# PEER value rows: gathered as 32 picks of 4 tokens and summed by TensorE alone, in place of 8 picks of 128 tokens summed by TensorE and VectorE

## The chip, the cores and the metric

One core of a Trainium2 chip runs the whole program, a two-block network over 512 tokens, in one launch. The time is that of the device, in microseconds. Three runs of the kernel before gave 4364.2 us in the median (4360.43 to 4366.75). PE is TensorE, DVE is VectorE, ACT is ScalarE, POOL is GpSimd, SP is SyncE.

## The reference, cut to what matters

Everything that changes lies in the last stage, the PEER feed-forward of the second block. Per token it takes 16 experts in each of 8 heads, 128 picks, out of 16384, and needs one row of 1024 floats from each of two tables in HBM per pick:

```python
def peer_ffn(h, w_q, keys1, keys2, u, v):          # tokens in chunks of 128
    q = (hc @ w_q).reshape(-1, 8, 128)
    s1, s2 = q[..., :64] @ k1.T, q[..., 64:] @ k2.T           # 128 keys each
    v1, i1 = lax.top_k(s1, 16); v2, i2 = lax.top_k(s2, 16)
    cand_s = v1[..., :, None] + v2[..., None, :]              # 256 per head
    cand_i = i1[..., :, None] * 128 + i2[..., None, :]
    best_s, best_pos = lax.top_k(cand_s, 16)
    expert = take_along_axis(cand_i, best_pos)
    g = softmax(best_s)
    act = gelu(einsum('cd,chkd->chk', hc, u[expert]))         # first table
    return einsum('chk,chkd->cd', g * act, v[expert])         # second table
# after it: x + gate2 * peer, and the final rms norm
```

## The kernel before, in words

Up to about 2975 us the program runs the first block and the attention of the second. Then `peer_stage` runs until the end. It holds 512 tokens as 4 tiles (`TT`) of 128 tokens. A tile has 128 picks per token, in 16 groups (`NG`) of `B` = 8 picks. One indirect DMA, which GpSimd issues, brings one pick of 128 tokens: 128 rows of 4 KB, token p's row in partition p. Both tables need 512 of them, 1024 in all.

The rows land in `peer_ring`, which has 16 slots, used as 4 places of 4 picks. Half a group (q = 0 or 1, 4 picks) is the unit of the list `order`, which fixes the order of all gathers. Entry i of it uses place i mod 4, and `free(i)` lets GpSimd refill a place only when the readers of entry i - 4 are done.

- A "first" entry (table `peer_u`) is read by VectorE: `dot_rows` multiplies each row by the token's input and sums it into `acts` (L3412), one instruction for each pick.
- A "value" entry (table `peer_v`) is read by two engines. TensorE (`add_rows`, L3213) takes 3 of 4 picks: the stationary operand is a 128x128 diagonal matrix with the weights of that pick, which ScalarE makes (`make_diags`, L3314), and the two 512-wide halves of the row stream past it into two PSUM banks. VectorE (`sum_rows`, L3443) takes the fourth with a multiply-add into two other banks. In the last 3 groups VectorE takes two of four.

Both engines are in the path of `free` for value entries. Group n of the values follows group n + 6 of the first rows (`LEAD`), less where a step carries two value groups (`EXTRA`), so 3 value groups are left when the first rows are over. The weight of a pick is gate times gelu(dot), made by VectorE a group at a time (`weigh`, L3424).

Beside that run, in each engine's written order: at the start, the last projections and norms of tiles 1 to 3 and the first choice; the query products of tiles 1 to 3 (`later_query` 0 to 7, L3173), 0 to 3 ahead of the first value rows and 4 to 7 between them; the key scores of the next tile (`scores`, on TensorE, copied out by ScalarE in `take_scores`); and the choice of the next tile's experts on VectorE (`choose`, in pieces, `choose_on`). At a tile's end `finish` adds the two partial sums, multiplies by the gate, adds to h and normalises.

Of the kernel before, what the change touches and what calls it, by code (L numbers as in the profile page):

```python
# [14 lines left out]
F32 = mybir.dt.float32  # L15
# [30 lines left out]
N_PEER = 16384  # L46
PICKS = PEER_HEADS * PEER_K
# [78 lines left out]
class Signal:  # L126
# [29 lines left out]
    i_weighed i_picked x_cum_stored x_cum_loaded x_logits x_masked x_exps x_turned x_taken y_added0 y_added1 y_added3  # L156
    y_weighed0 y_weighed1 stored x_copied_dve x_copied_act x_summed x_set x_inverse
# [2274 lines left out]
class ExpertKeys:  # L2432


    def __init__(self, S, st):
        H, NK = PEER_HEADS, PEER_K
        self.S, self.G = S, Routing()
        self.G.expert = S.sb("peer_expert", [P, TT, PICKS], I32, st)
        self.G.gate = S.sb("peer_gate", [P, TT, PICKS], F32, st)
# [18 lines left out]
    def choose(self, t, h0, h1):  # L2458
# [54 lines left out]
        for side in range(2):  # L2513
# [12 lines left out]
        nc.vector.scalar_tensor_tensor(key[:, 0, hs, :], key[:, 0, hs, :], float(P), key[:, 1, hs, :], ALU.mult,  # L2526
                                       ALU.add).then_inc(own.sem, o.up())
        self.dve.wait_ge(own.sem, o.value())
        nc.vector.tensor_copy(self.G.expert[:, t, :].rearrange("p (h k) -> p h k", h=H)[:, hs, :], key[:, 0, hs, :]).then_inc(self.chosen.sem, 1)
# [430 lines left out]
def peer_stage(S, K, qT, h2, M, mix, w_out, out_gain, out):  # L2960
# [6 lines left out]
    N, LEAD, EXTRA = TT * NG, 6, (20, 24, 28)  # L2967
    LAG, SCORED = LEAD - len(EXTRA), LEAD + 3
    queries_at = {LEAD + 1: (4, 5), LEAD + 2: (6, 7)}
    queries_out_at = {LEAD - 2: (0, 1), LEAD - 1: (2, 3), LEAD + 1: (4, 5), LEAD + 2: (6, 7)}  # L2970
    exps = S.sig("u_exps")
    acted, diags, w_staged, fin, cleared = (S.sig("y_" + x) for x in ("acted", "diags", "w_staged", "fin", "cleared"))
    arrived = [S.sig(f"y_arrived{q}", pool_dma=True) for q in range(4)]
    dotted = [S.sig(f"y_dotted{q}") for q in (0, 1)]
    added = [S.sig(f"y_added{q}") for q in (0, 1)]
    weighed = [S.sig(f"y_weighed{q}") for q in (0, 1)]
# [22 lines left out]
    def dve_rows(n):  # L2999
        return (0, 4) if n < N - LAG else (0, 2, 4, 6)  # L3000

    def pe_rows(n):
        return [b for b in range(B) if b not in dve_rows(n)]

    def pe_rows_to(n):
        return sum(len(pe_rows(x)) for x in range(n))

    def dve_rows_to(n, q):
        return sum(b // Q == q for x in range(n) for b in dve_rows(x))

    steps = [([m], []) for m in range(LEAD)]
    n_value = 0
    for m in range(LEAD, N):
        more = 2 if m in EXTRA else 1
        steps.append(([m], list(range(n_value, n_value + more))))
        n_value += more
# [7 lines left out]
    def slot_of(kind, n, b):  # L3024
        return Q * (place[kind, n, b // Q] % 4) + b % Q
# [753 lines left out]
```

## Time and profile before

| | |
|---|---|
| median of 3 runs | 4364.2 us (4360.43 to 4366.75) |
| the profiled execution: span from first to last instruction | 4359.8 us |
| mean granted TensorE clock in it | 0.927 |
| PE busy | 3776.8 us (87%) |
| DVE busy | 1707.1 us (39%) |
| ACT busy | 628.1 us (14%) |
| POOL busy | 1097.7 us (25%) |
| bytes moved | 1092.57 MB, mean 251 GB/s |

The profile gives no time of its own for the profiled execution beside the span. The span lies 4.4 us below the median of the runs and 0.6 us below the fastest. The busy shares are means over stages with different limits; the stage that changes is the last third, in which GpSimd issues the gathers. A matmul of float32 operands shows as two records of MATMUL and two of LDWEIGHTS, called passes below.

### The profile page before, as it was taken

How to read it: one execution, taken by the hardware profiler on the slowest of the kernel's cores; microseconds unless marked ns; L12 is line 12 of the kernel's file. 1: busy time of each engine (PE TensorE's matmuls, PEld its weight loads, DVE VectorE, ACT ScalarE, POOL GpSimd, SP SyncE). 2: the span in 40 equal slices, each digit the busy share in tenths (PEclk: the TensorE clock that was granted, in tenths of full speed). 3: DMA queues.
4: the chain of work that ended last, by engine and by line, in shares of the span. 5: the costliest groups of instructions: out<-in, count | busy, mean ns of one | idle time of the engine just before them, and what ended most of it. 6: DMA issues, size and time to landing. Idle time of an engine off the chain costs nothing. (4 is left out here: it accounts for less than half of the span.)

```text
span 4359.8 us, 45503 instructions
## 1 busy us (share of the span) xinstructions
PE 3776.8 (87%) x17106; PEld 2506.1 (57%) x17106; DVE 1707.1 (39%) x3683; ACT 628.1 (14%) x1566; POOL 1097.7 (25%) x1162
## 2 busy tenths in 40 slices
PE   7989999998989999999999997998766767766676
PEld 3455777744747888888999993475322223222222
DVE  2052231013730000000000004748778776877655
ACT  1121000013520000000000003143211111111011
POOL 0010000001400000000000000004567777777775
PEclk9989999999989999999999998988888888888888
DMA  3143675230019888898777754026899999999998
GB/s 113 48 153 123 237 251 191 98 135 0 20 63 277 307 295 304 306 312 294 259 254 256 246 203 138 30 97 243 339 353 388 418 416 420 415 418 418 412 420 355
DMA packets 546999, 1092.57 MB, mean 251 GB/s; under 512 B 37497, under 2 KB 333830, under 8 KB 546742
## 3 DMA queue, kind: packets, MB, share of 16 engines
q1 hardware_dynamic: 393674, 539.66, 36.5%
q0 software_dynamic: 150768, 546.25, 31.2%
q10 hardware_dynamic: 2428, 5.03, 0.3%
q8 instruction: 69, 1.13, 0.1%
q14 instruction: 60, 0.49, 0.0%
HBM read 1069.55 MB, written 21.30 MB: 250 GB/s over the span
## 5 line engine op out<-in xcount | busy, mean ns | idle before, releaser
L3213 PE MATMUL banks<-peer_ring,consts 128*128 128x512 f32 x1512 | 843.7, 719 | 375.3 <-DMA peer_ring<-in_peer_v_dram,peer_expert 375.3
L3213 PEld LDWEIGHTS banks<-peer_ring,consts 128*128 128x128 f32 x1512 | 337.8, 231 | 876.2 <-DMA peer_ring<-in_peer_v_dram,peer_expert 468.0
L3412 DVE SCALAR_TENSOR_TENSOR peer_ring<-peer_ring,banks 128x1024 f32<-128x1024 f32 x512 | 594.1, 1218 | 254.0 <-DMA peer_ring<-in_peer_u_dram,peer_expert 253.0
L3117 POOL DMA_INDIRECT peer_ring<-in_peer_u_dram,peer_expert x512 | 484.9, 947 | 552.2 <-POOLq L2744 346.9
L3117 POOL DMA_INDIRECT peer_ring<-in_peer_v_dram,peer_expert x512 | 488.7, 955 | 182.7 <-issue 139.8
L2013 DVE TENSOR_TENSOR experts_hid<-experts_gs,banks 128x128 f32<-128x128 f32 (+1 forms) x224 | 66.7, 298 | 1175.9 <-ACT experts_gs L1983 1175.9
L1890 PEld LDWEIGHTS banks<-rows_xt,experts_wg 128*128 128x128 f32 x3584 | 446.9, 192 | 45.6 <-issue 45.4
L1890 PE MATMUL banks<-rows_xt,experts_wg 128*128 128x128 f32 (+1 forms) x3584 | 462.3, 282 | 11.8 <-DMA experts_wu<-in_moe_w_up_dram 9.7
L1890 PE MATMUL banks<-rows_xt,experts_wu 128*128 128x128 f32 (+1 forms) x3584 | 460.9, 282 | 0.0
L1890 PEld LDWEIGHTS banks<-rows_xt,experts_wu 128*128 128x128 f32 x3584 | 440.7, 192 | 0.0
L405 PE MATMUL banks<-xT,proj_w 128*128 128x512 f32 (+1 forms) x720 | 319.9, 602 | 8.1 <-PEq L3563 4.6
L1799 POOL DMA_DIRECT2D rows_index<-token_of_row x13 | 7.5, 577 | 1060.3 <-PE banks L1815 1042.6
L1907 PE MATMUL banks<-experts_wd,experts_hid 128*128 128x512 f32 x560 | 251.9, 592 | 0.0
L405 PEld LDWEIGHTS banks<-xT,proj_w 128*128 128x128 f32 (+1 forms) x720 | 135.6, 190 | 185.2 <-issue 183.8
L1023 POOL TENSOR_TENSOR hgrn_both<-k,hgrn_diff 128x256 f32<-128x256 f32 x56 | 44.4, 814 | 776.0 <-ACT hgrn_diff L934 761.5
L1983 ACT ACTIVATE experts_gs<-banks 128x128 f32<-128x128 f32 (+1 forms) x224 | 64.0, 286 | 1182.8 <-PE banks L1890 1182.8
L3443 DVE SCALAR_TENSOR_TENSOR banks<-peer_ring,peer_wgt,banks 128x1024 f32<-128x1024 f32 x130 | 167.4, 1288 | 89.2 <-DMA peer_ring<-in_peer_v_dram,peer_expert 88.6
L1920 PE MATMUL banks<-experts_hid,experts_wd 128*128 128x152 f32 x1344 | 180.5, 293 | 0.0
L1920 PEld LDWEIGHTS banks<-experts_hid,experts_wd 128*128 128x128 f32 x1344 | 176.3, 190 | 0.4
L408 PE MATMUL banks<-proj_w,xT 128*128 128x512 f32 (+1 forms) x448 | 174.1, 548 | 0.0
L1357 PE MATMUL banks<-xT,ffn_wg 128*128 128x256 f32 x704 | 161.2, 382 | 1.2 <-ACT ada_c L1395 1.2
L1431 DVE TENSOR_TENSOR ffn_hid<-ffn_gs,banks 128x256 f32<-128x256 f32 x44 | 18.5, 422 | 360.8 <-ACT ffn_gs L1401 360.8
(502 smaller groups left out, 3766.7 us busy)
## 6 DMA issues: line engine op xcount, KB each, us to landing
experts_wg<-in_moe_w_gate_dram SPq DMA_DIRECT2D x112, 1024.0 KB, 5.1
experts_wu<-in_moe_w_up_dram SPq DMA_DIRECT2D x112, 1024.0 KB, 7.6
experts_wd<-in_moe_w_down_dram SPq DMA_DIRECT2D x112, 1024.0 KB, 8.0
ada_w<-in_w_ada_dram SPq DMA_DIRECT2D x12, 2048.0 KB, 8.0
ffn_wg<-in_ffn_w_gate_dram SPq DMA_DIRECT2D x22, 1024.0 KB, 7.8
ffn_wu<-in_ffn_w_up_dram SPq DMA_DIRECT2D x22, 1024.0 KB, 10.4
ffn_wd<-in_ffn_w_down_dram SPq DMA_DIRECT2D x22, 1024.0 KB, 11.8
y_rows<-blank SPq DMA_DIRECT2D x1, 12288.0 KB, 42.6
```

The costliest lines, as they stand in the source:

```text
L405: last = nc.tensor.matmul(out_of(g), wk[:, m * P:m * P + width], xT[:, k, :], start=(k == 0), stop=(k == KD - 1))
L408: last = nc.tensor.matmul(out_of(g), xT[:, k, m * P:(m + 1) * P], wk[:, 0:n], start=(k == 0), stop=(k == KD - 1))
L1357: last = nc.tensor.matmul(ps[bank][:, 0:ROWS], w[:, b, k, j * P:(j + 1) * P], xT[:, k, u * ROWS:(u + 1) * ROWS], start=(k == 0), stop=(k = ...
L1890: ins = nc.tensor.matmul(ps[bank][:, 0:E.rows], w[:, b, k, j * P:(j + 1) * P], E.xu[:, k, :], start=(k == 0), stop=(k == KD - 1))
L1907: ins = nc.tensor.matmul(ps[hf][:, :], hid[:, j, 0:P], wd[:, b, j, hf * 512:(hf + 1) * 512], start=(first and j == 0), stop=(final and j = ...
L1920: ins = nc.tensor.matmul(ps[d // 2][:, at:at + B.rows], wd[:, b, j, d * P:(d + 1) * P], hid[:, j, :], start=False, stop=False, skip_group_ ...
L1983: nc.scalar.activation(gs[:, j, 0:E.rows], ps[4 + j][:, 0:E.rows], ACT.Silu).then_inc(E.gated[j].sem, 1)
L2013: nc.vector.tensor_tensor(hid[:, j, 0:E.rows], gs[:, j, 0:E.rows], ps[6 + j][:, 0:E.rows], ALU.mult).then_inc(E.hidden[j].sem, 1)
L3117: pool.indirect_dma_start(out=ring[:, slot_of(kind, n, b), :], out_offset=None, in_=tables[kind == "value"], in_offset=bass.IndirectOffset ...
L3213: last = nc.tensor.matmul(ps[bank + hf][:, :], diag[:, n % 2 * B + b, :], ring[:, slot_of("value", n, b), hf * 512:(hf + 1) * 512], start= ...
L3412: nc.vector.scalar_tensor_tensor(row, row, 1.0, rows_at, ALU.mult, ALU.mult, accum_out=acts[:, t % 2, at:at + 1]).then_inc(dotted[q].sem, 1)
L3443: ins = nc.vector.scalar_tensor_tensor(sum_at, row, weight(n, b), sum_at, ALU.mult, ALU.add)
```

## The change

Value rows are gathered in another shape, and TensorE alone sums them.

- A tile's 128 picks are 4 portions of 32. One gather now brings 32 picks of 4 tokens: partition 32r + k holds pick k of the portion, of the unit's r-th token. A unit is 4 such gathers (g = 0..3), 16 tokens. 8 units make a portion, and 128 units make all four tiles, so the number of gathers stays 512, each of 128 rows.
- For that the pick numbers and the weights must be turned so that picks lie in the partitions. `choose` writes the numbers as floats, 4 times side by side (`expert_f`). TensorE transposes them (`turn_numbers`, L3203) and VectorE copies the four quarters out (`take_numbers`, L3457) to `rows_of`, from which the gather takes its row numbers. `weigh` makes a portion's weights, also 4 times side by side. TensorE transposes them (`turn_weights`, L3213 of the kernel after), and ScalarE writes them (`spread_weights`) into `spread`, blocks of 128x32 that are zero except for the weights. GpSimd zeroes `spread` once, after its first 16 gathers.
- `add_rows` multiplies, for each g, such a 128x32 block with the row's two halves. The result goes to partitions 32g to 32g + 31 of the two sum banks: column group g of TensorE, first half, second half, then group g + 1.
- VectorE's `sum_rows`, the copy and the add in `finish`, the diagonals and the zero matmuls that opened a tile are gone. `LEAD` is 5, each step from 5 on has 2 value units, and 10 units are left when the first rows are over.

The diff, cut to its core:

```diff
+    N, LEAD, SCORED = TT * NG, 5, 9
+    queries_at = {6: (4, 5), 7: (6, 7)}
+    queries_out_at = {3: (0, 1), 4: (2, 3), 6: (4, 5), 7: (6, 7)}
+    SHARE, PER_TILE = PEER_SHARE, 4
+    UNITS = P // (SHARE * Q)
...
     steps = [([m], []) for m in range(LEAD)]
     for m in range(LEAD, N):
+        steps.append(([m], [2 * (m - LEAD), 2 * (m - LEAD) + 1]))
+    steps += [([], [v, v + 1]) for v in range(2 * (N - LEAD), n_values, 2)]
...
                         else:
-                            pool.wait_ge(added[q].sem, added[q].at(n + 1))
-                            pool.wait_ge(weighed[q].sem, weighed[q].at(dve_rows_to(n + 1, q)))
+                            pool.wait_ge(added.sem, added.at(n + 1))
...
+                    if i == 4:
+                        pool.wait_ge(ready.sem, ready.at(2 * TT))
+                        nc.gpsimd.memset(spread, 0.0).then_inc(zeroed.sem, 1)
...
+                        p, c = n // UNITS, n % UNITS
+                        if c == 0:
+                            pool.wait_ge(numbers_out.sem, numbers_out.at(SHARE * (p + 1)))
+                        free(i)
+                        for g in range(Q):
+                            at = g * UNITS + c
+                            pool.indirect_dma_start(out=ring[:, slot_of(kind, n, g), :], out_offset=None, in_=tables[1],
+                                                    in_offset=bass.IndirectOffsetOnAxis(ap=rows_of[:, p % 2, at:at + 1], axis=0),
+                                                    ).then_inc(arrived[i % 4].sem, 16)
...
+                def add_rows(v):
...
+                    for g in range(Q):
+                        at = (g * UNITS + c) * 32
+                        for hf in range(2):
+                            last = nc.tensor.matmul(ps[bank + hf][32 * g:32 * g + 32, :], spread[:, p % 2, at:at + 32],
+                                                    ring[:, slot_of("value", v, g), hf * 512:(hf + 1) * 512], start=first,
+                                                    stop=last_of, skip_group_check=True)
+                    last.then_inc(added.sem, 1)
...
                 for n in range(4):
                     later_query(n)
+                for m in range(2, len(steps)):
...
+                    if m % 4 == 2 and m < N:
+                        turn_numbers(m // 4)
...
                 choose_on(1)
-                dot_group(4)
-                choose_on(3)
-                dot_group(5)
+                take_numbers(0)
+                for m in range(4, len(steps)):
```

What GpSimd issues from the start of the stage, before (L3117 is every gather; the table's name tells first rows from values):

```order
L3117 DMA peer_ring<-in_peer_u_dram,peer_expert 128x1024 x52
L3117 DMA peer_ring<-in_peer_v_dram,peer_expert 128x1024 x4
L3117 DMA peer_ring<-in_peer_u_dram,peer_expert 128x1024 x4
L3117 DMA peer_ring<-in_peer_v_dram,peer_expert 128x1024 x4
```

and what it issues there now, the first value gather waiting for the turned numbers:

```order
L3104 DMA peer_ring<-in_peer_u_dram,peer_expert 128x1024 x16
L3095 MEMSET consts 128x2048
L3104 DMA peer_ring<-in_peer_u_dram,peer_expert 128x1024 x28
L3114 DMA peer_ring<-in_peer_v_dram,value_rows 128x1024 x4
L3104 DMA peer_ring<-in_peer_u_dram,peer_expert 128x1024 x4
L3114 DMA peer_ring<-in_peer_v_dram,value_rows 128x1024 x4
```

The first value gather has moved from place 53 to place 45.

VectorE at the end of the first norms, before: dots of group 3, the join and norm of tile 3, one piece of choosing, dots of group 4:

```order
L3412 SCALAR_TENSOR_TENSOR peer_ring,peer_act<-peer_ring,banks 128x1024 x8
L3382 TENSOR_TENSOR peer_acc<-banks,mod_rows 128x512
L3384 TENSOR_TENSOR h<-h,peer_acc 128x512
L3374 TENSOR_SCALAR tail_ss<-tail_ss 128x1
L3377 RECIPROCAL tail_ss<-tail_ss 128x1
L2482 CAST peer_f<-peer_i 128x64
L2483 TENSOR_TENSOR xT<-peer_v 128x2x256
L2489 MAX peer_best<-xT 128x8 x2
L2492 MAX_INDEX peer_at<-peer_best,xT 128x8 x2
L2498 MATCH_REPLACE xT<-peer_best,xT 128x256 x2
L3412 SCALAR_TENSOR_TENSOR peer_ring,peer_act<-peer_ring,banks 128x1024 x8
```

and after, from the same piece of choosing on:

```order
L2483 CAST peer_f<-peer_i 128x64
L2484 TENSOR_TENSOR xT<-peer_v 128x2x256
L2490 MAX peer_best<-xT 128x8 x2
L2493 MAX_INDEX peer_at<-peer_best,xT 128x8 x2
L2499 MATCH_REPLACE xT<-peer_best,xT 128x256 x2
L3457 CAST value_rows<-banks 32x32 x4
L3433 SCALAR_TENSOR_TENSOR peer_ring,peer_act<-peer_ring,banks 128x1024 x4
L3384 TENSOR_REDUCE peer_total<-peer_gate 128x2
L3386 RECIPROCAL peer_total<-peer_total 128x2
L3388 TENSOR_TENSOR peer_gate<-peer_gate,peer_total 128x32
L3446 TENSOR_TENSOR peer_wgt<-peer_act,peer_gate 128x128
L3433 SCALAR_TENSOR_TENSOR peer_ring,peer_act<-peer_ring,banks 128x1024 x4
```

The four copies L3457, which wait for TensorE's transpose, now stand ahead of the dots of group 4.

TensorE from the end of the first norms, before (L3173 are the query products, 8 for each of `later_query`; L3136 the scores; L3213 the value rows):

```order
L3150 MATMUL banks<-consts,later_xT 128x128 x8
L3173 MATMUL banks<-later_xT,mix 128x384 x32
L3201 MATMUL banks<-peer_zero 128x512 x2
L3213 MATMUL banks<-peer_ring,consts 128x512 x24
L3173 MATMUL banks<-later_xT,mix 128x384 x16
L3213 MATMUL banks<-peer_ring,consts 128x512 x12
L3173 MATMUL banks<-later_xT,mix 128x384 x16
L3136 MATMUL banks<-consts,proj_w 128x128 x16
L3213 MATMUL banks<-peer_ring,consts 128x512 x84
```

and after (L3175 the query products, L3203 and L3213 the two transposes, L3229 the value rows, L3138 the scores):

```order
L3152 MATMUL banks<-consts,later_xT 128x128 x8
L3175 MATMUL banks<-later_xT,mix 128x384 x32
L3203 MATMUL banks<-consts,peer_expertf 128x128
L3213 MATMUL banks<-consts,peer_wgt 128x128
L3229 MATMUL banks<-peer_ring,consts 32x512 x32
L3203 MATMUL banks<-consts,peer_expertf 128x128
L3175 MATMUL banks<-later_xT,mix 128x384 x16
L3229 MATMUL banks<-peer_ring,consts 32x512 x16
L3175 MATMUL banks<-later_xT,mix 128x384 x16
L3229 MATMUL banks<-peer_ring,consts 32x512 x8
L3213 MATMUL banks<-consts,peer_wgt 128x128
L3229 MATMUL banks<-peer_ring,consts 32x512 x8
L3138 MATMUL banks<-consts,proj_w 128x128 x16
```

The transpose of the first numbers stands behind the first four query products, and a half group of 4 picks is 8 matmuls where it was 6.

## Rows read from the trace of the kernel before

**Rows 1.** The page's groups: line, engine, shapes, count | busy us, mean ns | idle before.
```profile
L3213 PE MATMUL banks<-peer_ring,consts 128*128 128x512 f32 x1512 | 843.7, 719 | 375.3 <-DMA peer_ring<-in_peer_v_dram,peer_expert 375.3
...
L3412 DVE SCALAR_TENSOR_TENSOR peer_ring<-peer_ring,banks 128x1024 f32<-128x1024 f32 x512 | 594.1, 1218 | 254.0 <-DMA peer_ring<-in_peer_u_dram,peer_expert 253.0
L3117 POOL DMA_INDIRECT peer_ring<-in_peer_u_dram,peer_expert x512 | 484.9, 947 | 552.2 <-POOLq L2744 346.9
...
L3443 DVE SCALAR_TENSOR_TENSOR banks<-peer_ring,peer_wgt,banks 128x1024 f32<-128x1024 f32 x130 | 167.4, 1288 | 89.2 <-DMA peer_ring<-in_peer_v_dram,peer_expert 88.6
```

**Rows 2.** Windows: stretch, length, busy us (count) by engine, PEclk, DMA share, GB/s.
```profile
3200.00:3300.00 100.00, 62.05 (x107) 24.37 (x105) 95.48 (x289) 7.89 (x28) 64.92 (x69) 0.81 0.92 360
...
4200.00:4300.00 100.00, 68.39 (x121) 26.96 (x120) 58.76 (x94) 9.85 (x35) 74.31 (x80) 0.85 1.03 420
```

**Rows 3.** Waits, 2976 to 3300 us: who waited for whom, us, times, longest.
```profile
POOL peer_ring L3117 <- DVE peer_ring L3412: 52.7, 10, 9.8
...
POOL peer_ring L3117 <- PE banks L3213: 21.0, 5, 12.7
```

**Rows 4.** Waits, 3300 to 4300 us.
```profile
POOL peer_ring L3117 <- PE banks L3213: 12.6, 20, 1.4
```

**Rows 5.** Timeline of POOL: start, us, instruction, [idle before <-releaser].
```profile
2976.31 0.94 POOL L3117 DMA_INDIRECT peer_ring<-in_peer_u_dram,peer_expert  x1 [346.85 <-POOLq L2744]
...
3044.89 0.94 POOL L3117 DMA_INDIRECT peer_ring<-in_peer_u_dram,peer_expert  x1 [0.30 <-issue]
...
3091.81 0.94 POOL L3117 DMA_INDIRECT peer_ring<-in_peer_u_dram,peer_expert  x1 [9.78 <-DVE peer_ring L3412]
...
3177.94 0.94 POOL L3117 DMA_INDIRECT peer_ring<-in_peer_v_dram,peer_expert  x1 [12.68 <-PE banks L3213]
```

**Rows 6.** Timeline of SP's queue, DVE, PE, 3051 to 3087 us.
```profile
3051.64 1.22 DVE L3412 SCALAR_TENSOR_TENSOR peer_ring<-peer_ring,banks 128x1024 f32<-128x1024 f32 x1
...
3052.79 1.22 DVE L3412 SCALAR_TENSOR_TENSOR peer_ring<-peer_ring,banks 128x1024 f32<-128x1024 f32 x1
...
3056.79 37.00 SPq L3090 DMA_DIRECT2D mix<-in_w_peer_q_dram  x2
...
3070.17 23.22 PE L3173 MATMUL banks<-later_xT,mix 128*128 128x384 f32 x64 [13.41 <-DMA mix<-in_w_peer_q_dram]
...
3086.77 0.21 DVE L3424 TENSOR_TENSOR peer_wgt<-peer_act,peer_gate 128x48 f32<-128x48 f32 x1 [8.91 <-ACT peer_act L3303]
```

**Rows 7.** The page's DMA issues: count, KB each, median us to landing.
```profile
ada_w<-in_w_ada_dram SPq DMA_DIRECT2D x12, 2048.0 KB, 8.0
```

**Rows 8.** Chain that ended last, 4244 to 4272 us: start, us, what.
```profile
4244.24 7.13 PE banks L3213 x12
...
4255.36 8.81 DMA peer_ring<-in_peer_v_dram,peer_expert
4264.22 8.07 PE banks L3213 x12
```

**Rows 9.** Windows of line L3213 alone: PE, PEld, PEclk, DMA share, GB/s.
```profile
4184.20:4187.60 3.40, 3.40 (x5) 1.35 (x4) 0.50 1.02 418
4254.20:4258.70 4.50, 4.47 (x11) 2.08 (x12) 1.00 1.03 421
4274.20:4278.70 4.50, 4.50 (x11) 2.11 (x12) 1.00 1.03 421
```

**Rows 10.** Timeline of PE, 97 to 105 us: a stationary block of 16 columns.
```profile
97.69 7.04 PE L405 MATMUL banks<-xT,proj_w 128*16 128x512 f32 x16
```

**Rows 11.** Window inside it, columns as in Rows 2.
```profile
100.00:104.00 4.00, 4.00 (x11) 0.87 (x9) 0.00 (x0) 0.00 (x0) 0.00 (x0) 1.00 0.41 139
```

**Rows 12.** Timeline, the end of the kernel.
```profile
4337.11 0.94 POOL L3117 DMA_INDIRECT peer_ring<-in_peer_v_dram,peer_expert  x1 [0.30 <-issue]
...
4344.92 3.70 PE L3213 MATMUL banks<-peer_ring,consts 128*128 128x512 f32 x8 [1.29 <-DMA peer_ring<-in_peer_v_dram,peer_expert]
...
4352.75 1.06 ACT L3321 ACTIVATE mix<-h 128x1024 f32<-128x1024 f32 x1 [23.36 <-DVE h L3461]
```

More of the change, by code:

```diff
@@ L46 @@
 N_PEER = 16384
+PEER_SHARE = 4
 PICKS = PEER_HEADS * PEER_K
@@ L2997, in exps_at @@
         return signal.at(part + 1 if t == 0 else len(parts) + t)
[L2999 to L3009, printed above, removed]
+    n_values = TT * PER_TILE * UNITS
     steps = [([m], []) for m in range(LEAD)]
[L3012 removed]
     for m in range(LEAD, N):
[L3014 to L3017 removed]
+        steps.append(([m], [2 * (m - LEAD), 2 * (m - LEAD) + 1]))
+    steps += [([], [v, v + 1]) for v in range(2 * (N - LEAD), n_values, 2)]
     order = []
     for firsts, values in steps:
[L3020 to L3021 removed]
+        for q in range(2):
+            order += [("first", n, q) for n in firsts]
+            order += [("value", v, 0) for v in values[q:q + 1]]
     place = {x: i for i, x in enumerate(order)}
     def slot_of(kind, n, b):
[L3025 removed]
+        return Q * (place[kind, n, b // Q if kind == "first" else 0] % 4) + b % Q
     def arrival(kind, n, q):
@@ L3204, in add_rows @@
-                def add_rows(n):
-                    bank = sum_banks(n // NG)
-                    for q in range(2):
-                        pe.wait_ge(*arrival("value", n, q))
-                        for b in pe_rows(n):
-                            if b // Q != q:
-                                continue
-                            pe.wait_ge(diags.sem, diags.at(pe_rows_to(n) + pe_rows(n).index(b) + 1))
-                            for hf in range(2):
-                                last = nc.tensor.matmul(ps[bank + hf][:, :], diag[:, n % 2 * B + b, :],
-                                                        ring[:, slot_of("value", n, b), hf * 512:(hf + 1) * 512], start=False,
-                                                        stop=(n % NG == NG - 1 and b == pe_rows(n)[-1]), skip_group_check=True)
-                        last.then_inc(added[q].sem, 1)
+                pe.wait_ge(zeroed.sem, zeroed.at(1))
@@ new lines, in take_numbers @@
+                def take_numbers(p):
+                    dve.wait_ge(numbers_turned.sem, numbers_turned.at(p + 1))
+                    if p >= 2:
+                        dve.wait_ge(added.sem, added.at(UNITS * (p - 1)))
+                    for r in range(SHARE):
+                        rows = slice(32 * r, 32 * r + 32)
+                        to = rows_of[rows, p % 2, :].rearrange("p (g x) -> p g x", g=Q)
+                        src = ps[2][rows, 0:P].rearrange("p (g x) -> p g x", g=Q)[:, :, UNITS * r:UNITS * (r + 1)]
+                        nc.vector.tensor_copy(to, src).then_inc(numbers_out.sem, 1)
@@ L3454, in finish @@
[L3454 to L3460 removed]
+                    dve.wait_ge(fin.sem, fin.at(2 * t + 1))
@@ L3533, in _ @@
                     choose_on(1 if t else 2 if m > SCORED and m % 2 == 0 else 3)
-                    if not any(n % NG == 0 for n in values):
-                        next(finishing, None)
                 for piece in finish(TT - 1):
```

268 lines of the change are left out of this document (120 added, 148 removed).

## The prediction

> **What bounds the kernel now.** I read the windows first. From 3300 us to the end GpSimd issues 80 gathers in 100 us, window after window, at 418 to 420 GB/s, and the 16 DMA engines are busy throughout (share 1.03) [rows 2]. A gather costs GpSimd 0.94 us and 0.30 us of idle "issue" behind it [rows 1, 5, 8], 1.243 us in all. The first starts at 2976.31 and the last at 4337.11 [rows 5, 12]: 1360.8 us for 1023 steps, of which 1271.6 are cadence and 89.2 are lost. The change leaves the 1024 gathers and their rows of 4 KB as they are, so 1271.6 us is a floor, and less than 90 us can be won even if every wait goes.
>
> Where the 89 go is told by the waits. Before 3300 us GpSimd waits 52.7 us for the dots of VectorE and 21.0 for TensorE [rows 3]; after it 12.6 us in 20 waits for TensorE, half of which is the 0.30 that stands between any two gathers [rows 4]. So the steady stage is paced by GpSimd and the DMA engines, TensorE being just in time, and the start of the stage is paced by VectorE (95% busy from 3200 to 3300 [rows 2]).
>
> Just in time means this. A value batch of 4 takes 3.7 us from its first to its last issue, 8.8 us from there until it has landed, and TensorE 7.1 to 8.1 us [rows 8]. That is 19.6 to 20.6 us, and its place in the ring is wanted again after 16 x 1.243 = 19.9.
>
> **The change part by part.**
>
> *VectorE.* 130 multiply-adds of 1.29 us go [rows 1], 167 us, about 2.6 us in each 19.9. After 3300 us this buys nothing, since nobody waited there. It helps only while the experts of tile 1 are chosen, from 3200 to 3300.
>
> *The front.* Here a wait is added. The first value gather now waits for numbers that TensorE turns, and the order of TensorE puts that transpose behind query products 0 to 3, which wait for 2 MB of weights. VectorE waits too, with its copies ahead of the dots of group 4, which ran at 3051.64 before. The weights are asked for at 3056.79 and used at 3070.17, 13.4 us later, with the gathers beside them [rows 6]. GpSimd will stand still there now, so I take the 8.0 us of such a load elsewhere [rows 7]: 3064.8. The four products took 23.2 us [rows 6], which gives 3088.0, and the transpose and four small copies about 2 (an estimate from VectorE's 0.21 us [rows 6] for such a size): 3090. The bounds are 3088 and 3096. By then 44 gathers are out, the 44th at about 3043.6, a step before 3044.89 [rows 5]. Before, 64 were out by 3091.81 [rows 5]. From there to the last issue 1245.3 us passed for 959 steps, 53.3 of them lost. The kernel after has 980 gathers to go.
>
> *GpSimd's zeroing of 2048 columns.* No row shows its like. VectorE passes over 1024 columns in 1.22 us [rows 1], so 2.4 us at its speed and 24 at a tenth of it; both lie under the standstill that ends at 3090. Price nothing.
>
> *TensorE.* Four picks are 8 matmuls, 16 passes, where they were 6 matmuls and 12 passes. A pass of 512 columns takes 0.427 us at 2.4 GHz (11 in 4.5 us at a granted clock of 1.00) and 0.855 us at 1.2 GHz (4 in 3.4 us at 0.50) [rows 9]. A stationary block of 16 columns saves nothing: 16 passes in 7.04 us [rows 10]. So 16 passes one after another are 7.0 us at the full clock. If the second half of one column group runs beside the first half of the next, three passes of 16 are hidden and it is 5.6 us. No row shows two matmuls beside each other, so I keep both ends, and I take 7.0, the value of the nearest row.
>
> The Trainium skill ("TensorEngine Tiling (Array Packing)", Key Properties) says that tiles operate independently and that different ones can run LdWeights and Matmul in parallel. No run here shows it. By that rule the batch would be the 5.6 us, which is the first rival below.
>
> *The clock.* Before, it fell between batches (mean 0.85 [rows 2]). A batch that came 2.9 us after the end of another (4251.4 to 4254.2) and one that came 1.9 us after (4272.3 to 4274.2) ran wholly at 2.4 GHz [rows 8, 9]. With 7.0 us of work in 9.94 the idle is 2.9, so I expect it mostly high. That narrow blocks keep it high is shown by 7 us of 16 columns with 1.00 granted [rows 10, 11]. That they can raise it once fallen is not shown.
>
> *Steady stage.* Room for TensorE is 19.9 - 3.7 - 8.8 = 7.4 us against 7.0. Before, 12.6 us were waited for TensorE here [rows 4], and single gathers ran longer than 0.94 (mean 0.947 [rows 1]). I keep 15.
>
> *From 3090 to 3300.* Walking the rings, with dots at 1.14 us each (3051.64 to 3052.79, also the step of all the others [rows 6]) and 7.0 us a batch: 6 us for VectorE, which comes out of its wait with two groups of dots and three pieces of choosing undone; 6.5 and 5 us where query products 4 to 7 (two take 11.6, half of 23.2) stand between batches, since 14 + 11.6 exceeds 19.9; and 10 us at step 9, where the second scores wait for ScalarE's copy, which waits for VectorE's dots. Before, that place cost 12.7 [rows 5]. For the choice of tile 1 I leave 4 of the 14 that 69 gathers in place of 80 cost from 3200 to 3300 [rows 2], and 4 for the two later tiles, where a batch now stands behind the score copies. Together 36. The bounds are 15 (all but step 9 absorbed) and 60.
>
> *The end.* 10 value batches are left when the first rows are over, and they come every 4.97 us while TensorE needs 7.0. From the first issue of the last batch before them: 3.7 + 8.8 + 7.0 = 19.5, ten batches 69.5, multiply and add 2.5, and the 7.05 us from 4352.75 to the end of the span [rows 12]: 98.5. Here the bounds are 5.6 (84) and 7.0.
>
> *Sum.* 3090, plus 936 steps to that issue (1163.4), plus 36 + 15, plus 98.5 = 4402.9. Against the profiled 4359.8 that is +43. The profiled span lies 4.4 us under the median, so I put it on the median: 4364.2 + 43 = 4407. What was bought is 53 us of waits less 51; what is paid is 20 gathers at the front less 1.8 us (23), and the tail.
>
> **The rivals.**
>
> 1. *Halves of neighbouring groups overlap.* 5.6 us a batch: the end is 14 us shorter, the front loses about 10 less, the steady stage 2. 4403 - 26 = 4377, on the median 4381. For it: the blocks lie in different columns. Against it: the idle grows to 4.3 us, and then the clock falls as it does now, which takes the gain back in the steady stage. Chance 0.27.
>
> 2. *The clock stays at 1.2 GHz under narrow blocks.* 16 passes are 13.7 us, above the 9.94 at which batches come, so TensorE becomes the bound: 128 x 13.7 = 1753 from about 3102, some 25 for the products between, 10 behind: 4890. With three passes hidden, 128 x 11.1: 4560. For it: full blocks lose the clock now, and these use a quarter of the columns. Against it: rows 10 and 11. Chance 0.12.
>
> 3. *TensorE misses the room in every round.* If each batch begins at 1.2 GHz as the 7.13 us ones do, four more passes make it 8.8 against 7.4, 1.4 us in each of some 52 rounds: +75, 4482. Against it: a batch of 8.8 leaves 1.1 us of idle, after which the clock is high; and slower issue shortens the 8.8 us of landing. Chance 0.11.
>
> 4. *Faster than before.* VectorE's relief decides. With rival 1's passes and the waits from 3090 to 3300 at their lower bound of 15 (VectorE's debt of dots absorbed by its new 2.6 us a step, query products caught up at once) and 5 steady: 3090 + 1163 + 20 + 84 = 4357, on the median 4361; with the waits gone to 10 and the restart at 3088 it is 4354. It decides from a total of waits under 16 us. For it: 52.7 us of waits for dots were there to be taken [rows 3]. Against it: 36 of the 89 us were lost before 3091.81 (115.5 us for 64 steps [rows 5]), where the new wait stands anyway. Chance 0.10.
>
> The forecast itself has 0.40.
>
> **How the numbers follow.** 4407 is the likeliest case, with its own range from 4385 (front 15) to 4435 (front 60). From 4364 to 4495 lie the forecast, rival 1, rival 3 and the upper part of 4; left out are 0.12 for the clock and some 0.08 below. A change of under 0.2%, 8.7 us, can't be told from none. Slower by more: the forecast, 1 (nearly all), 2 and 3, less a part for errors in the hand-walked front: 0.79. Within: 0.09. Faster: 0.12.
>
> **What would show it.** Right: GpSimd idle over 40 us before its first gather of `value_rows`, VectorE too; TensorE records of the 32-wide blocks 0.43 us apart; 80 gathers in 100 us in the middle; the last ten batches 7 us apart. Rival 1 shows as batches 5.6 us apart in the end, rival 2 as a granted clock near 0.5, rival 3 as fewer than 78 gathers in 100 us with waits for TensorE. Wrong at its root would be a first value gather before 3080, or more than 80 gathers in 100 us.

## The result, and the profile after

| | before | after |
|---|---|---|
| median of 12 runs | 4361.8 us (4359.6 to 4366.8) | 4371.0 us (4368.2 to 4375.0) |
| profiled span | 4359.8 us | 4370.8 us |
| mean granted TensorE clock | 0.927 | 0.862 |
| PE busy, DVE busy | 3776.8, 1707.1 us | 3385.1, 1541.5 us |

The ratio is 1.0022, with a 95% interval of 1.0014 to 1.0029: 9.2 us slower, where 43 were forecast. The direction held and the size did not. The profiled spans differ by 11.0.

The page's groups after, to be read beside [rows 1]. The 130 multiply-adds of VectorE have no successor, as forecast. The value rows are 2048 matmul records of 128*32 blocks in place of 1512, and yet their busy time is 441.5 us where it was 843.7:

```profile
L3229 PE MATMUL banks<-peer_ring,consts 128*32 128x512 f32 x2048 | 441.5, 1005 | 743.7 <-DMA peer_ring<-in_peer_v_dram,value_rows 737.8
L3433 DVE SCALAR_TENSOR_TENSOR peer_ring<-peer_ring,banks 128x1024 f32<-128x1024 f32 x512 | 594.2, 1217 | 439.3 <-DMA peer_ring<-in_peer_u_dram,peer_expert 438.6
```

2048 passes one after another need 874 us even at 2.4 GHz (0.427 each, [rows 9]), and the line has half of that: passes run at the same time. (The mean length of a record says less. In the kernel before 1512 of 719 ns would add up to 1087 us, and they lie in 843.7.) That one line holds most of the error of the forecast.

The windows, columns as in [rows 2]:

```profile
3200.00:3300.00 100.00, 35.53 (x176) 8.14 (x173) 75.61 (x245) 2.68 (x10) 67.68 (x72) 0.62 0.92 361
4200.00:4300.00 100.00, 37.15 (x167) 7.17 (x163) 47.41 (x85) 1.91 (x9) 74.45 (x80) 0.53 1.03 420
```

VectorE has gone from 95% to 76% busy from 3200 to 3300, GpSimd from 69 gathers to 72. From 4200 to 4300 TensorE has gone from 68% busy to 37%, and the clock from 0.85 to 0.53, and GpSimd still issues 80 gathers at 420 GB/s.

GpSimd's waits from 2976 to 3300 us, as [rows 3]:

```profile
POOL peer_ring L3114 <- DVE value_rows L3457: 44.3, 1, 44.3
...
POOL peer_ring L3104 <- DVE peer_ring L3433: 24.7, 6, 6.5
...
POOL peer_ring L3114 <- PE banks L3229: 9.8, 1, 9.8
```

The new wait is the first line. Beside it the waits for dots have fallen from 52.7 to 24.7 us and those for TensorE from 21.0 to 9.8. Part of the first fall is the window alone: the standstill pushes gather 200 and its wait for dots (6.4 us, at 3311.62) behind 3300. From 3300 to 4300 TensorE is not waited for any more (0.6 us against the 12.6 of [rows 4]). The dots of VectorE are, for 11.9 us in 12 waits, 6.4 of them at gather 200 and half a microsecond in each of the others:

```profile
POOL peer_ring L3104 <- DVE peer_ring L3433: 11.9, 12, 6.4
...
POOL peer_ring L3114 <- PE banks L3229: 0.6, 2, 0.3
```

The standstill in the timeline, to be read beside [rows 5, 6]: the load of the query weights, the query products 0 to 3, the transpose, the four copies, the first value gather.

```profile
3056.73 31.26 SPq L3074 DMA_DIRECT2D mix<-in_w_peer_q_dram  x2
...
3065.06 22.53 PE L3175 MATMUL banks<-later_xT,mix 128*128 128x384 f32 x64 [8.36 <-DMA mix<-in_w_peer_q_dram]
...
3087.43 0.27 PE L3203 MATMUL banks<-consts,peer_expertf 128*128 128x128 f32 x1
...
3087.80 0.84 DVE L3457 CAST value_rows<-banks 32x32 int32<-32x32 f32 x4 [36.25 <-PE banks L3203]
...
3088.92 0.94 POOL L3114 DMA_INDIRECT peer_ring<-in_peer_v_dram,value_rows  x1 [44.30 <-DVE value_rows L3457]
```

It starts again at 3088.92 (forecast 3090), with the load used 8.3 us after it was asked for (forecast 8.0) and products of 22.5 us (forecast 23.2).

TensorE's batches, one in the steady stage and one in the last ten, with the weight loads of the first:

```profile
4207.45 3.66 PE L3229 MATMUL banks<-peer_ring,consts 128*32 128x512 f32 x16 [6.32 <-DMA peer_ring<-in_peer_v_dram,value_rows]
...
4343.12 1.95 PE L3229 MATMUL banks<-peer_ring,consts 128*32 128x512 f32 x16 [1.38 <-DMA peer_ring<-in_peer_v_dram,value_rows]
```

```profile
4207.45 0.23 PEld L3229 LDWEIGHTS banks<-peer_ring,consts 128*32 128x32 f32 x8 [8.06 <-DMA peer_ring<-in_peer_v_dram,value_rows]
...
4208.31 0.22 PEld L3229 LDWEIGHTS banks<-peer_ring,consts 128*32 128x32 f32 x4 [0.63 <-issue]
...
4209.16 0.22 PEld L3229 LDWEIGHTS banks<-peer_ring,consts 128*32 128x32 f32 x4 [0.64 <-issue]
```

16 passes take 3.66 us, which is four passes of 0.855 us (1.2 GHz, [rows 9]) and 0.24 more; and 1.95 us, four of 0.427 (2.4 GHz) and 0.24. The weight loads start in bursts 0.86 us apart, one pass at 1.2 GHz, with four loads to a burst after the first. The single records of the trace say the same: four passes start from 4207.45 to 4207.49, the next four from 4208.30. So four passes run at a time, one in each column group. (A block of a column group also writes to 32 partitions of its own in PSUM; the two can't be told apart here.)

### The profile page after: what moved, and what is told of

It is laid out like the page before. It is cut to its first block and busy times, and to the rows that moved or that the text cites. A ratio compares the mean times of both kernels' runs of the same rounds, so it can differ in the third digit from the quotient of the medians.

```text
span 4370.8 us, 45812 instructions
## 1 busy us (share of the span) xinstructions
PE 3385.1 (77%) x17663; PEld 2258.2 (52%) x17666; DVE 1541.5 (35%) x3567; ACT 528.6 (12%) x1252; POOL 1097.7 (25%) x1163
## 5 line engine op out<-in xcount | busy, mean ns | idle before, releaser
L3229 PE MATMUL banks<-peer_ring,consts 128*32 128x512 f32 x2048 | 441.5, 1005 | 743.7 <-DMA peer_ring<-in_peer_v_dram,value_rows 737.8
L3229 PEld LDWEIGHTS banks<-peer_ring,consts 128*32 128x32 f32 x2048 | 84.6, 154 | 1050.6 <-DMA peer_ring<-in_peer_v_dram,value_rows 784.5
L3114 POOL DMA_INDIRECT peer_ring<-in_peer_v_dram,value_rows x512 | 489.4, 956 | 210.8 <-issue 153.8
L1357 PE MATMUL banks<-xT,ffn_wu 128*128 128x256 f32 x704 | 159.1, 379 | 0.0
L1367 PE MATMUL banks<-ffn_wd,ffn_hid 128*128 128x512 f32 x352 | 154.7, 592 | 0.0
```

The costliest lines, as they stand in the source:

```text
L1357: last = nc.tensor.matmul(ps[bank][:, 0:ROWS], w[:, b, k, j * P:(j + 1) * P], xT[:, k, u * ROWS:(u + 1) * ROWS], start=(k == 0), stop=(k = ...
L1367: last = nc.tensor.matmul(ps[2 * s + half][:, :], hid[:, j, s * P:(s + 1) * P], wd[:, b, j, half * 512:(half + 1) * 512], start=(g == 0 an ...
L3114: pool.indirect_dma_start(out=ring[:, slot_of(kind, n, g), :], out_offset=None, in_=tables[1], in_offset=bass.IndirectOffsetOnAxis(ap=rows ...
L3229: last = nc.tensor.matmul(ps[bank + hf][32 * g:32 * g + 32, :], spread[:, p % 2, at:at + 32], ring[:, slot_of("value", v, g), hf * 512:(hf ...
```

## The experiments

"Lost" is the time of GpSimd's gathers above 1.243 us each; gathers are numbered from 0, and number 44 is the first value gather of the kernel after. The stage itself begins at 2970.3 to 2977.6 us in these profiles, whatever was changed behind that point, so "lost" compares two of them better than a time of day does.

**1. The numbers turned ahead of the query products.**

```diff
+                turn_numbers(0)
                 for n in range(4):
                     later_query(n)
...
-                    if m % 4 == 2 and m < N:
+                    if m % 4 == 2 and 2 < m < N:
```

> The changed kernel with one move: TensorE turns the first pick numbers ahead of query products 0 to 3 instead of behind them. Theory A (the 44 us in which GpSimd stood still before its first value gather are what the change costs, against some 30 us that it wins later): the first value gather is issued near 3058 in place of 3088.9, the third value batch then waits for TensorE until about 3095 (gather 60 of 1024, which the changed kernel reaches near 3115), and the time falls by about 20 us, to about 4351, some 10 under the kernel before. Theory B (the time is set later, by the DMA engines at 418 to 420 GB/s and by the end of the kernel, and a gap at the start is made up): within 4 us of the changed kernel, 4371.

Measured: 4346.1 us, ratio to before 0.9965 (0.9951 to 0.9978). The first value gather:

```profile
3057.47 0.94 POOL L3114 DMA_INDIRECT peer_ring<-in_peer_v_dram,value_rows  x1 [15.08 <-DVE value_rows L3458]
```

The gather comes 31.5 us earlier, 1.9 of which is the earlier beginning of the stage in this execution, and the kernel ends 25 us earlier (4371.0 less 4346.1). The rest goes to a 5.2 us wait for TensorE at gather 60, where the values now stand behind the query products. Theory A held, with 5 us more won than it said. So the place of the transpose is what made the change slower. With it moved, the same change is 0.35% faster than the kernel before.

**2. All value matmuls in one column group.**

```diff
-                            last = nc.tensor.matmul(ps[bank + hf][32 * g:32 * g + 32, :], ...
+                            last = nc.tensor.matmul(ps[bank + hf][0:32, :], ...
```

> The changed kernel with all four stationary blocks of a value batch put into column group 0 (output partitions 0 to 31), so its sums are not the reference's; the number and size of matmuls, gathers and waits are the same. It asks why 16 passes took 3.7 us at 1.2 GHz where I had reckoned 5.6 to 7.0 at 2.4. Theory C (four column groups work beside each other, whatever the written order): a batch is now 16 passes one after another, 6.9 us at 2.4 GHz and 13.7 at 1.2, and the kernel takes about 4403, as I forecast for such batches, or up to 4890 if the clock stays low. Theory D (a pass with a 32-column block is itself cheaper, or overlaps its neighbour in any column group): batches stay at 3.7 us and the time at 4371.

Measured: 4411.7 us, ratio 1.0115 (1.0096 to 1.0133). The last nine batches stand as one block, and GpSimd waits for each:

```profile
4340.19 61.99 PE L3229 MATMUL banks<-peer_ring,consts 128*32 128x512 f32 x144
```

```profile
4354.39 0.94 POOL L3114 DMA_INDIRECT peer_ring<-in_peer_v_dram,value_rows  x1 [2.19 <-PE banks L3229]
...
4361.25 0.94 POOL L3114 DMA_INDIRECT peer_ring<-in_peer_v_dram,value_rows  x1 [2.20 <-PE banks L3229]
```

144 passes in 61.99 us are 0.430 each, 6.9 us a batch, and the batches' first gathers are 6.86 us apart. From gather 980 (4313.18) to the end of the span 98.5 us pass, the forecast's figure to a tenth. TensorE is waited for where query products 4 to 7 stand between batches, too, by about what was forecast (6.5 and 5):

```profile
3156.09 0.94 POOL L3114 DMA_INDIRECT peer_ring<-in_peer_v_dram,value_rows  x1 [4.85 <-PE banks L3229]
...
3180.96 0.94 POOL L3114 DMA_INDIRECT peer_ring<-in_peer_v_dram,value_rows  x1 [5.27 <-PE banks L3229]
```

Theory C held. This is the kernel that the prediction described, 5 us from its 4407, and part of that closeness is luck: between gathers 44 and 980 it loses 65.0 us, where the forecast had 51, but its stage begins 6.0 us earlier than in the profile that the forecast started from. So the tail and the query products were priced rightly for serial batches; the batches were not serial. The halves of one group's row go to two banks and yet don't overlap here, so different banks alone are not enough.

**3. Two column groups** (`32 * (g % 2)` in the same place), timed once.

> As the run before, with the blocks alternating between column groups 0 and 1 (sums again not the reference's). Theory C: 8 passes one after another in each group, so 6.9 us a batch at 1.2 GHz and 3.5 at 2.4, under the 7.4 us of room, and a time within 10 us of 4371. Theory D: 3.7 us at 1.2 GHz. If groups overlap only where one follows another in the written order (my rival 1), a batch has 13 passes, 5.6 us at 2.4 GHz.

Measured: 4369.9 us. A batch in the steady stage, and one in the end:

```profile
4204.34 6.05 PE L3229 MATMUL banks<-peer_ring,consts 128*32 128x512 f32 x16 [4.07 <-DMA peer_ring<-in_peer_v_dram,value_rows]
...
4340.00 3.65 PE L3229 MATMUL banks<-peer_ring,consts 128*32 128x512 f32 x16 [1.33 <-DMA peer_ring<-in_peer_v_dram,value_rows]
```

3.65 us is eight passes of 0.427 and 0.23: two at a time. (The 6.05 us batch ran in part at either level, at a mean granted clock of 0.59.) Theory C held. At two groups the time is already that of four (4371.0), since a batch comes every 4.97 us in the end and every 9.94 before. TensorE's speed beyond that buys nothing. Nor does the lower clock of the kernel after cost anything behind 3300 us: GpSimd waits 0.6 us for TensorE there.

**4. The written order turned round: first halves of groups 0 to 3, then second halves**, timed once.

```diff
-                    for g in range(Q):
-                        at = (g * UNITS + c) * 32
-                        for hf in range(2):
+                    for hf in range(2):
+                        for g in range(Q):
+                            at = (g * UNITS + c) * 32
```

> The changed kernel with the 8 matmuls of a batch written in the order first half of groups 0 to 3, second half of groups 0 to 3, where it was both halves of a group in turn. Theory A (a matmul runs beside those of the other three column groups whatever the written order, since 16 passes took 3.66 us at 1.2 GHz, four times 0.855 plus the fill): the batch stays at 3.6 to 3.7 us at 1.2 GHz and 1.9 to 2.0 at 2.4, and the time at 4371, give or take 4. Rival (only neighbours in the written order overlap, and the order decides how many): the batch gets shorter than 3.4 us at 1.2 GHz, or longer than 4.3, and the time moves with the tail, ten batches.

Measured: 4372.0 us.

```profile
4216.62 3.64 PE L3229 MATMUL banks<-peer_ring,consts 128*32 128x512 f32 x16 [6.08 <-DMA peer_ring<-in_peer_v_dram,value_rows]
```

3.64 us against 3.66, as Theory A had it. Within these eight matmuls the order doesn't matter. The forecast's first rival had let the groups overlap only where one follows the other. The two orders would then have differed, and they don't.

**5. Full 128x128 blocks, and VectorE's share given to TensorE: the kernel before with `dve_rows` empty.**

> The kernel before with one part of the change alone: TensorE sums all 8 picks of a group with its 128x128 diagonals, VectorE sums none; gathers stay 8 picks of 128 tokens. A half group is 16 passes one after another. Theory A with C: VectorE is relieved as in the change and the first value gather does not wait for turned numbers, but TensorE needs 7.0 us (at 2.4 GHz) to 8.8 us (3.4 us of it at 1.2 GHz) in 7.4 us of room, and 7.0 in the 4.97 us of the end: 20 to 90 us slower than before, 4382 to 4450. If taking VectorE out is what counts and TensorE's batch time does not: 10 to 20 us faster than before, 4345 to 4352.

Measured: 4383.5 us, ratio 1.0047 (1.0031 to 1.0062), 22 us above before.

```profile
3182.75 0.93 POOL L3116 DMA_INDIRECT peer_ring<-in_peer_v_dram,peer_expert  x1 [16.04 <-PE banks L3212]
```

```profile
4339.53 37.50 PE L3212 MATMUL banks<-peer_ring,consts 128*128 128x512 f32 x87
```

GpSimd waits 16.0 us for TensorE at step 9 (12.7 before, [rows 5]), and the last batches stand end to end, 0.431 us a pass. The waits from 2976 to 3300 us, beside [rows 3]:

```profile
POOL peer_ring L3116 <- DVE peer_ring L3411: 45.2, 8, 9.8
POOL peer_ring L3116 <- PE banks L3212: 27.9, 5, 16.0
```

VectorE is relieved here just as in the change, and the relief is there: 7.5 us less are waited for dots. TensorE takes 6.9 of them back, and in the last stretch, from gather 980 to the end, 90.7 us pass where it was 77.3. Full blocks run one at a time, so the relief doesn't pay. That it pays in the change because narrow blocks overlap in four groups follows from this run and experiment 2 together; no run has full blocks that overlap.

**6. VectorE's load put back into the kernel after.**

```diff
+                        if n >= LEAD and b == q * Q:
+                            nc.vector.tensor_reduce(extra[:, 2 * n + q:2 * n + q + 1], row, mybir.AxisListType.X, ALU.add)
                         nc.vector.scalar_tensor_tensor(row, row, 1.0, rows_at, ...
```

> The changed kernel with VectorE's load put back: ahead of the first dot of each half group from group 5 on it sums a row of 1024 elements into a column that nobody reads (110 reductions of some 1.1 to 1.3 us, two in each 19.9 us; before, 130 multiply-adds of 1.29 us). TensorE sums all values as in the changed kernel. Theory A (the relief of VectorE is what made the stage from 3100 to 3300 us lose less than it did before; the waits for dots there are paid one for one): the losses of GpSimd between gather 56 and gather 200 grow by 8 to 20 us, nearly all for VectorE, and the time is 4380 to 4390, ratio to before 1.0045 to 1.0065. Theory B (the relief bought nothing, since TensorE's shorter batches did): 4371, give or take 4, with the same losses at the same gathers.

Measured: 4381.0 us, ratio 1.0045 (1.0028 to 1.0061), 10 us above the kernel after. The added operations from 3100 to 3300 us, and GpSimd's waits there:

```profile
L3435 DVE TENSOR_REDUCE extra_sums<-peer_ring 128x1 f32<-128x1024 f32 x18 | 21.9, 1218 | 39.5 <-DMA peer_ring<-in_peer_u_dram,peer_expert 39.4
```

```profile
POOL peer_ring L3105 <- DVE peer_ring L3436: 17.1, 3, 7.7
...
POOL peer_ring L3115 <- PE banks L3230: 9.7, 1, 9.7
```

The same stretch of the kernel after has 12.5 us of waits for dots. The losses at gathers 56, 152, 168 and 200 grow from 17.7 to 24.8 us, by 7.1, just under the 8 that the expectation gave as its lower end; the rest of the 10 is spread over the stage, and 2.4 of it lie before gather 45, where nothing was added yet. The time is inside Theory A's range. In all 118 reductions of 1.22 us were put back, 144 us against the 167 of [rows 1]. So the relief is worth 8 to 10 us here.

**7. LEAD 6, with the copies of the numbers moved behind the dots of group 4**, on top of experiment 1.

```diff
-    N, LEAD, SCORED = TT * NG, 5, 9
+    N, LEAD, SCORED = TT * NG, 6, 9
...
-                take_numbers(0)
                 for m in range(4, len(steps)):
...
+                    if m == 4:
+                        take_numbers(0)
```

> Numbers turned ahead of the query products (as in e1_numbers_first, 4346.1), and in addition LEAD 6 (one more group of first rows ahead of the first values) and VectorE's copies of the numbers moved behind the dots of group 4, so that VectorE's debt of dots is not paid while GpSimd stands. Theory A (what GpSimd stands still before 3300 us comes back one for one): of the 14.8 us lost ahead of the first value gather and 6.2 us behind it some 4 to 8 are won net, since value units left for the tail are more by two: 4338 to 4343, ratio to before 0.994 to 0.996. Theory B (past some point the DMA engines pace the ring, and earlier gathers only wait later): 4345 to 4350, with new waits for VectorE or TensorE of the same sum from 3100 to 3300 us.

Measured: 4345.5 us, no gain over experiment 1 (4346.1). Before the first value gather 7.1 us are lost and not 14.8, but 6.6 are lost at gather 48 in exchange, and 11.6 and not 9.9 at step 9. The wait was VectorE's debt of dots, and it only changed its name. Theory A fell. The time is B's, but its cause is not shown: the new waits lie ahead of 3100 us, at gathers 48 (6.6) and 64 (4.9), both for VectorE, and not in the stretch where B looked for them.

**8. ScalarE's copies of the second scores put ahead of its activation at step 9**, on top of experiment 1.

```diff
+                    if m == SCORED:
+                        take_scores(1, 0)
+                        take_scores(1, 1)
...
-                        if m == at:
+                        if m == at and tt > 1:
```

> Numbers turned ahead of the query products (as in e1_numbers_first, 4346.1), and ScalarE's two copies of the second scores put ahead of its activation at step 9, so that TensorE's second scores, and the values behind them, don't wait for VectorE's dots of that step. Theory A: the 9.9 us that GpSimd waited for TensorE at gather 124 go and come back at the end: 4335 to 4338, ratio 0.9935 to 0.9945. Theory B (GpSimd is then caught by VectorE's dots, which are late by as much): the loss at 124 goes but 5 us or more appear before gather 200: 4341 to 4346.

Measured: 4337.1 us, ratio 0.9945 (0.9929 to 0.9961). TensorE in experiment 1 and here:

```profile
3174.64 2.08 PE L3138 MATMUL banks<-consts,proj_w 64*128 64x128 f32 x16 [15.94 <-ACT xT L3263]
```

```profile
3156.28 1.16 PE L3138 MATMUL banks<-consts,proj_w 64*128 64x128 f32 x16 [1.21 <-ACT xT L3263]
```

The 9.9 us at gather 124 are gone, and the median is 9.0 lower (in the two profiles 7.1 us less are lost in all). Theory A held.

**9. All moves, and the choice of tile 1 begun a step earlier and spread in single pieces (SCORED 8).** 

```diff
-                    choose_on(1 if t else 2 if m > SCORED and m % 2 == 0 else 3)
+                    choose_on(1 if t else 2 if m > SCORED else 3)
```

> The three moves together (numbers turned first with LEAD 6 and the copies behind the dots of group 4; the second scores copied out first), and the scores of tile 1 a step earlier, its choice spread over seven steps in single pieces. Theory A (losses before 3300 us add): 4325 to 4332, ratio 0.9915 to 0.993, and GpSimd's loss against 1.243 us a gather from the first value gather to gather 200 under 15 us where the changed kernel lost 27. Theory B (VectorE's work before 3300 us, 1.14 us a dot and the choice, is the bound whatever the order): 4338 to 4346, with the waits moved to other gathers, 20 us or more of them for VectorE.

Measured: 4333.7 us, ratio 0.9935 (0.9920 to 0.9949), just above A's range. A's second figure failed: from the first value gather, number 52 here, to gather 200 GpSimd loses 29 us (22 without the wait ahead of number 52), not under 15. Ahead of gather 100 nothing was won (43.3 us lost, 42.3 in experiment 8); from 101 to 200 5.8 us are lost, most of it at 128 and 192, where the kernel after lost 21.

**10. The same without LEAD 6 and the move of the copies.**

> The kernel of e8_all_moves without LEAD 6 and without the move of the number copies: e6_scores_first (4337.1) with the scores of tile 1 a step earlier and its choice spread in single pieces. Theory A (the 3.4 us between e6_scores_first and e8_all_moves come from the spread choice, LEAD 6 being worth nothing as it was from e1_numbers_first to e5_numbers_first_lead6): 4332 to 4335, with 14 to 15 us lost ahead of the first value gather and under 8 between gathers 100 and 200. Theory B (both are needed): 4336 to 4339.

Measured: 4332.1 us, ratio 0.9932 (0.9916 to 0.9949), equal to experiment 9. GpSimd's waits from 3100 to 3300 us:

```profile
POOL peer_ring L3114 <- PE banks L3229: 4.5, 1, 4.5
POOL peer_ring L3104 <- DVE peer_ring L3437: 1.6, 1, 1.6
```

Theory A held: 14.7 us are lost ahead of the first value gather, and between gathers 100 and 200 7.1 where experiment 8 lost 12.6. LEAD 6 is worth nothing, the earlier and spread choice some 5 us; the intervals of experiments 8 and 10 overlap, so for the 5 us the gathers speak and not the ratio. Part of them goes to a new wait, the 4.5 us for TensorE at gather 108; the waits for dots at 152, 168 and 200, 11 us in experiment 8, are down to 1.2. This version and that of experiment 9 are the best, 27 and 30 us under the kernel before of the same rounds.

## Why the prediction was wrong

**The step that failed is the time of TensorE's batch.** The prediction bounded it by 5.6 us (three passes of 16 hidden) and 7.0 (none), and took 7.0 as "the value of the nearest row". It is 1.95 us at 2.4 GHz and 3.66 at 1.2, because four column groups work at once. Both bounds were wrong: the lower one let only neighbours in the written order overlap, and no row spoke for such a limit. The prediction's own steps with 1.8 us (a quarter of 7.0): the end becomes 49.7 for ten batches at 4.97, plus 3.7, 8.8, 1.8, 2.5 and 7.05, 73.6 in place of 98.5, and the 15.5 us for query products and later tiles go. That is 4402.9 - 40.4 = 4362.5, 8 below the profiled 4370.8, and 7.5 of these 8 are the choice of tile 1, the other term that was too small. Experiment 2 shows that the batch time carries the miss: with serial batches the kernel takes 4411.7, 40.7 more.

The sum again, with what each term measured (profiled span, 4402.9 forecast, 4370.8 measured):

| step | forecast | measured | through |
|---|---|---|---|
| restart at the first value gather | 3090 | 3088.9 | |
| VectorE's debt behind it | 6 | 6.2 | gather 56 |
| query products 4 to 7 between batches | 11.5 | 0 | batch time |
| the second scores at step 9 | 10 | 9.5 | gather 124 |
| choice of tile 1 | 4 | 11.5 | gathers 152, 168, 200 |
| two later tiles | 4 | 0 | batch time |
| the rest | 15 | 13.5 | |
| gather 980 to the end of the span | 98.5 | 77.7 | batch time |

The terms sum to 32 us less than forecast: 20.8 in the tail, 10.2 in the losses, 1.1 at the restart.

**The tail.** The ten last batches were to come 7.0 us apart. They come 4.95 to 5.01 apart, as fast as GpSimd issues them, and the end is cadence, one landing, one batch and what follows:

```profile
4347.36 0.94 POOL L3114 DMA_INDIRECT peer_ring<-in_peer_v_dram,value_rows  x1 [0.30 <-issue]
```

```profile
4358.06 3.18 PE L3229 MATMUL banks<-peer_ring,consts 128*32 128x512 f32 x16 [3.01 <-DMA peer_ring<-in_peer_v_dram,value_rows]
```

**The query products.** "14 + 11.6 exceeds 19.9" was the reason for 11.5 us of waits. With batches of 3.7 it is 7.4 + 11.6 = 19.0, which doesn't exceed it, and no wait appeared.

**Step 9.** Right in size and in cause: TensorE's second scores waited 16.68 us for ScalarE's copy, and GpSimd 9.83 for the values behind them. Experiment 8 took it away.

```profile
3199.29 2.08 PE L3138 MATMUL banks<-consts,proj_w 64*128 64x128 f32 x16 [16.68 <-ACT xT L3262]
```

```profile
3205.29 0.94 POOL L3114 DMA_INDIRECT peer_ring<-in_peer_v_dram,value_rows  x1 [9.83 <-PE banks L3229]
```

**The choice of tile 1.** Under-sized, 4 against 11.5. The 2.6 us in each 19.9 that VectorE was given back are less than its burst of choosing at one place; the earlier and spread choice of experiment 10 won some 5 us of it. That the burst is the cause is the reading that fits these two runs; it was not tried alone.

**GpSimd's zeroing** took 1.82 us, below the 2.4 and 24 that bounded it, and was hidden, as priced.

```profile
2996.64 1.82 POOL L3095 MEMSET consts<- 128x2048 f32 x1
```

**The clock.** Forecast mostly high in the steady stage; it was 0.53 there. The reason given (idle of 2.9 us between batches) went with the batch time: a batch of 3.66 leaves 6.3 us. The second rival (the clock stays low) was thus half right in its cause and wrong in its price. It counted 16 passes one after another at 1.2 GHz; four at a time they fit into 9.94 us more than twice.

**Rivals.** The first named the right mechanism (overlap of groups) and a quarter of its size: three passes of 16 hidden, where twelve are. The third did not occur: no wait for TensorE over 0.3 us after 3300. The fourth (faster, by VectorE's relief and shorter batches) did not occur: the losses from gather 44 to 980 were 41 us, not the 20 it needed. Once the transpose is moved the kernel is faster than before, but by an earlier restart, with losses still of 46. Against the kernel before, the balance can be read at single gathers: number 64 is issued 28.7 us later (3120.48 against 3091.81 [rows 5]), number 200 14.4 later, the last one 10.3 later (4347.36 against 4337.11 [rows 12]). Of the 28.7 us of the standstill, 18.4 are given back. Experiment 6 puts 8 to 10 of them down to VectorE's relief. The rest was not measured alone. TensorE's shorter batches are the likely cause, since its waits at gathers 68 and 100 (2.8 and 3.9 us before) and nearly all of the 12.6 us behind 3300 are gone.

## What to carry to other kernels

When a new wait is added, look in each engine's written order for what stands ahead of the instruction that ends it: here one 0.27 us transpose behind 22.5 us of products cost more than all the rest of the change earned. A bound for an operation that no row shows must come from what the hardware could do at best (all four groups at once), not from the smallest step beyond the nearest row. And once a resource has slack, its speed and its clock are out of the sum: two column groups, in the one run that was timed, were as good as four.

## What was not expected of the hardware

- Matmuls of 128x32 blocks that go to four different column groups run four at a time: 16 float32 passes of 512 columns in 1.95 us at 2.4 GHz, 3.66 at 1.2; in two groups 3.65 at 2.4 GHz, and in the steady stage 6.05 at a mean clock of 0.59; in one 6.9 at 2.4 GHz. The order in which the groups' matmuls are written made no difference here (3.64 against 3.66).

The Trainium skill ("TensorEngine Tiling (Array Packing)", Key Properties) says that tiles operate independently and that different ones can run LdWeights and Matmul in parallel. These traces agree, with 16 passes in the time of 4. The sentence holds no limit to neighbours; the 5.6 us that the prediction drew from it took in such a limit.

- With shorter batches the granted clock was lower. From 4100 to 4300 us, with the same 80 gathers in 100 us, the mean granted clock was 0.58 with TensorE 37% busy (four groups), 0.69 with 60% (two) and 0.94 with 76% (one).

- A faster reader did not shorten the landing of its rows but let it grow. From the last issue of a value batch to its first matmul it was 8.9 us before (4255.36 to 4264.22 [rows 8]) and 11.4 after:

```profile
4206.07 0.93 POOL L3114 DMA_INDIRECT peer_ring<-in_peer_v_dram,value_rows  x1 [0.31 <-issue]
```

```profile
4217.44 1.10 PE L3229 MATMUL banks<-peer_ring,consts 128*32 128x512 f32 x4 [5.92 <-DMA peer_ring<-in_peer_v_dram,value_rows]
```

It grows slowly. Over all value batches issued from 3400 to 3500, from 3700 to 3800 and from 4100 to 4200 us the mean is 7.2, 8.4 and 11.4 us after, and 6.8, 8.0 and 8.1 before. A gather of 128 rows of 4 KB every 1.243 us asks for 422 GB/s and 420 are moved (an estimate; the difference would be 3 us in 700). So a backlog of rows is the likely reason: GpSimd asks for a little more than the DMA engines move, and before, its waits for TensorE took the backlog away. No run tried that alone. What ends the growth is the next reader. For the first rows issued from 4197.38 to 4201.10, 3.7 us of issues, 11.3 of landing and 4.65 of VectorE's four dots are 19.7 of the ring's 19.9, and GpSimd waits for the last dot:

```profile
4212.42 1.22 DVE L3433 SCALAR_TENSOR_TENSOR peer_ring<-peer_ring,banks 128x1024 f32<-128x1024 f32 x1 [5.33 <-DMA peer_ring<-in_peer_u_dram,peer_expert]
...
4217.35 0.93 POOL L3104 DMA_INDIRECT peer_ring<-in_peer_u_dram,peer_expert  x1 [0.35 <-DVE peer_ring L3433]
```

The 8.8 us that the prediction took for the landing was thus no constant, and the room of 7.4 us that it left for TensorE depends on how long the stage has run.
